# A hybrid decoder step: the first expert matrix transposed on chip beside the branches, so that 128 tokens fetch its rows and VectorE forms their products

## What is computed

```python
x = x + jnp.sum(gates * bproj, axis=2) @ w_out
x = x + peer(rmsnorm(x, norm_ffn), pk_wq, pk_k1, pk_k2, pk_u, pk_v)

def block(xb):                                   # peer, per block of 128 tokens
    q = (xb @ w_q).reshape(PK_BLOCK, PK_HEADS, 2, PK_DKEY // 2)
    s1 = jnp.einsum('thd,kd->thk', q[:, :, 0], sub_k1)
    s2 = jnp.einsum('thd,kd->thk', q[:, :, 1], sub_k2)
    v1, i1 = lax.top_k(s1, PK_TOPK)
    v2, i2 = lax.top_k(s2, PK_TOPK)
    ...
    top, pos = lax.top_k(cand, PK_TOPK)          # 16 of 256 sums, 8 heads: 128 experts a token
    eidx = jnp.take_along_axis(cidx, pos, axis=-1)
    gate = jax.nn.softmax(top, axis=-1)
    act = jax.nn.gelu(jnp.einsum('thkd,td->thk', u_tab[eidx], xb), approximate=False)
    return jnp.einsum('thk,thkd->td', gate * act, v_tab[eidx])
```

## Time and profile before

| what | value |
|---|---|
| median of 3 runs | 2785.19 us (2784.17 to 2786.49) |
| profiled execution, its own time | 2789.63 us |
| its span | 2787.7 us |
| TensorE busy | 2554.8 us, 92% of the span |
| VectorE busy | 1493.1 us, 54% |
| ScalarE busy | 801.3 us, 29% |
| GpSimd busy | 352.9 us, 13% |
| mean granted TensorE clock | 0.945 of full |

### The profile page before, as it was taken

The page is one execution under the profiler, slowest core; times in us unless marked ns, Lnnn a source line. Parts: engine busy times, 40 slices in busy tenths (PEclk is TensorE's granted clock), DMA queues, the critical chain, the costliest instruction groups (busy, mean ns, idle before and its releaser), DMA issues.

```text
span 2787.7 us, 46563 instructions
## 1 busy us (share of the span) xinstructions
PE 2554.8 (92%) x19385; PEld 2379.8 (85%) x19385; DVE 1493.1 (54%) x3427; ACT 801.3 (29%) x1147; POOL 352.9 (13%) x372
## 2 busy tenths in 40 slices
PE   7976886877769999998999999999999999999997
PEld 5954666865548998786999999999999999999997
DVE  3354375426222222376677566666412468778876
ACT  3221252210112112122232344444422333333332
POOL 2000000000000000000000000000000546667520
PEclk9987898978778999998999999999999999999998
DMA  4110320001313332220333346555644789999993
GB/s 133 48 38 23 96 62 2 4 4 48 122 45 87 81 83 85 62 79 23 136 132 136 132 137 190 169 165 165 182 151 148 268 277 341 353 345 345 344 348 122
DMA packets 267010, 398.09 MB, mean 143 GB/s; under 512 B 18641, under 2 KB 192737, under 8 KB 265265
## 3 DMA queue, kind: packets, MB, share of 16 engines
q1 hardware_dynamic: 222960, 274.07, 30.5%
q0 software_dynamic: 25408, 85.38, 8.4%
q10 hardware_dynamic: 18432, 35.66, 3.5%
HBM read 325.13 MB, written 69.92 MB: 142 GB/s over the span
## 4 chain that ended last, share of the span: by engine, by line
PE 87%; DVE 9%; issue 2%; ACT 2%; DMA 0%; DVEq 0%; ACTq 0%
PE PS L988 87%; DVE arena L1545 3%; ACT arena L644 1%; DVE arena L1557 1%; PE PS L992 1%; DVE arena L1739 1%; DVE rstd L1885 1%; ACT arena L648 0%; DVE arena L1551 0%; DVE rstd L1573 0%; DVE arena L1554 0%; ACT L644 0%; DMA XT<-in_xT 0%; DVE arena L1900 0%; DMA arena<-in_memkT 0%
## 5 line engine op out<-in xcount | busy, mean ns | idle before, releaser
L2007 DVE TENSOR_TENSOR LO<-RAW,HI 128x1024 fp32r<-128x1024 f32 x256 | 314.7, 1230 | 511.9 <-ACT HI L911 504.0
L911 ACT ACTIVATE HI<-RAW 128x1024 fp32r<-128x1024 f32 x256 | 271.0, 1059 | 918.5 <-PE PS L988 891.0
L988 PE MATMUL PS<-XH,HI 128*128 128x272 f32 x2048 | 429.2, 291 | 13.8 <-DVE LO L2007 13.8
L988 PE MATMUL PS<-XH,LO 128*128 128x272 f32 x2048 | 424.9, 289 | 0.0
L988 PE MATMUL PS<-XL,HI 128*128 128x272 f32 x2048 | 423.2, 288 | 0.0
L988 PE MATMUL PS<-HT,W 128*128 128x272 f32 (+1 forms) x1536 | 376.8, 407 | 18.6 <-DVE HT L1576 12.4
L988 PEld LDWEIGHTS PS<-HT,W 128*128 128x128 f32 (+1 forms) x1536 | 293.7, 193 | 95.7 <-issue 24.0
L988 PE MATMUL PS<-WH,HI 128*128 128x416 f32 x1024 | 360.0, 352 | 0.0
L988 PE MATMUL PS<-WL,HI 128*128 128x416 f32 x1024 | 359.3, 351 | 0.0
L988 PE MATMUL PS<-WH,LO 128*128 128x416 f32 x1024 | 357.2, 349 | 0.0
L988 PEld LDWEIGHTS PS<-XH,HI 128*128 128x128 f32 x2048 | 322.5, 189 | 14.1 <-issue 14.1
(11 more groups left out here) (272 smaller groups left out, 2940.6 us busy)
## 6 DMA issues: line engine op xcount, KB each, us to landing
RAW<-in_uT SPq DMA_DIRECT2D x128, 512.0 KB
RAW<-in_vT SPq DMA_DIRECT2D x128, 512.0 KB
table_a<-AX ACTq DMA_DIRECT2D x128, 272.0 KB, 2.1
W<-in_w_in SPq DMA_DIRECT2D x58, 512.0 KB, 4.0
gate_table<-GST SPq DMA_DIRECT2D x13, 2048.0 KB, 11.3
AIN<-table_a SPq DMA_DIRECT2D x128, 208.0 KB
GQ<-gate_table SPq DMA_DIRECT2D x32, 832.0 KB
W<-in_wq SPq DMA_DIRECT2D x16, 512.0 KB, 3.9
```

Source lines behind the costliest of these rows:

```text
L911: nc.scalar.activation(HI[:, s % NRING], RAW[:, s % NRING], ACT.Copy).then_inc(S("hi"), 1)
L988: return nc.tensor.matmul(out, lhsT, rhs, start=first, stop=last)
L2007: dve.tensor_tensor(LO_[:, s % NRING], RAW[:, s % NRING], HI[:, s % NRING].bitcast(F32), ALU.subtract).then_inc(S("lo"), 1)
```

## The change

- **Rows of u.** 128 tiles of u are loaded once more, on GpSimd's queue, turned on VectorE in blocks of 32x32 (`turn_tile`, one transpose of 128x1024), and written by GpSimd to a new table `u_rows` in DRAM (`turn_tiles`: four DMAs per tile, each from 32 partitions, in pieces of 1 KB). 18 tiles are turned in the mLSTM, 16 in the RWKV chunks, 10 in attention, 56 beside the gates and 28 beside the queries. One buffer in and one out serve the first two stages, two and two the others. Within each stage GpSimd does its tiles before the stage's other transfers (in the mLSTM before all outputs).
- **First pass for 416 tokens.** 24 matmuls of 416 columns per slot in the place of 48 of 272. The 128 tokens' own vectors are turned to rows (product `xt`, into XTOK); GpSimd gathers 128 rows of u for each (`gather_first`, three buffers), VectorE multiplies and sums (`dot`), ScalarE applies GELU (`picked`). `gather_act` goes.
- **One-hots split.** VectorE compares four tokens at once (two TENSOR_TENSOR of 128x512 per unit), ScalarE multiplies by the gates (`gated_hots`, four activations of 128x128 per unit). 104 units lie in 58 slots from slot 53 on (46 slots with two units, 12 with one) where it was two in each of 52. The parts of the choice take 10 slots per token tile, where it was 8; 16 dots lie beside them, the other 112 behind.
- Constants move into a block that is given up after the branches; some semaphores are merged.

```diff
+TILES = {"M": (0, 18, 1), "R": (18, 16, 1), "A": (34, 10, 2), "G": (44, 56, 2), "Q": (100, 28, 2)}
 def part_slot(t, part):
-    return 2 + 8 * t + part
+    return 2 + 10 * t + part
 def hots_slot(u):
-    return part_slot(NPT, 4) + u // 2
+    return part_slot(NPT - 1, 7) + 4 + u * 58 // (8 * NEB)
+def dotted_by(s):
+    first, even, early = part_slot(0, 7) + 5, part_slot(NPT - 1, 7) + 5, 16
+    if s < even:
+        return max(0, s - first) * early // (even - first)
+    return min(P, early + (s - even) * (P - early) // (NK - 2 - even))
...
 # GpSimd
+            def turn_tiles(phase):
+                first, n, depth = TILES[phase]
+                for i in range(first, first + n + depth):
+                    k = i - depth
+                    if k >= first:
+                        pool.wait_ge(S("tr"), k + 1)
+                        rows, turned = u_rows[k].rearrange("(b c) q x -> q c b x", b=4), tile_out[phase][(k - first) % depth]
+                        for q in range(4):
+                            pool.dma_start(rows[q], turned[32 * q:32 * q + 32].rearrange("c (b x) -> c b x", b=4)
+                                           ).then_inc(S(f"tout{k % 2}"), 16)
+                    if i < first + n:
+                        pool.dma_start(tile_in[phase][(i - first) % depth], a["uT"][:, i].rearrange("p k n -> p (k n)")
+                                       ).then_inc(S(f"tin{i % 2}"), 16)
+                for i in range(2):
+                    pool.wait_ge(S(f"tout{i}"), 64 * ((first + n + 1 - i) // 2))
+            turn_tiles("M")
             pool.wait_ge(S("ctail"), 8)
             pool.dma_start(o["conv"], CT).then_inc(S("out"), 16)
...
+            def gather_first(j):
+                if j >= NGU:
+                    pool.wait_ge(S("dot"), j - NGU + 1)
+                pool.indirect_dma_start(out=GU[j % NGU][0:NGT], out_offset=None, in_=flat_u,
+                                        in_offset=bass.IndirectOffsetOnAxis(ap=EIDX[0:NGT, 1, j:j + 1], axis=0)
+                                        ).then_inc(S(f"gr{j % NGU}"), 16)
...
 # ScalarE
+            def gated_hots(u):
+                act.wait_ge(S("oheq"), u + 1)
+                for x in range(4):
+                    hot = OH[:, u % NOH, 1, x]
+                    ins = nc.scalar.activation(hot, hot, ACT.Copy, scale=IT[:, 2, 4 * u + x:4 * u + x + 1])
+                ins.then_inc(S("oh1"), 1)
...
+                for u in units_at(hots_slot, s):
+                    gated_hots(u)
                 for u in units_at(copy_slot, s):
                     copy_unit(u)
...
 # TensorE, first_products
-                    ins = exact(ps, (HI[:, s % NRING, ks], LO_[:, s % NRING, ks]), (XH[:, k, :], XL[:, k, :]),
-                                k == 0, k == DT - 1)
+                    mul(ps, uh, XH[:, k, :], k == 0, False)
+                    mul(ps, uh, XL[:, k, :], False, False)
+                    ins = mul(ps, ul, XH[:, k, :], False, k == DT - 1)
...
 # VectorE
+            def turn_tile(phase):
+                ...
+                dve.wait_ge(S(f"tin{i % 2}"), 16 * (i // 2 + 1))
+                k = i - depth
+                if k >= first:
+                    dve.wait_ge(S(f"tout{k % 2}"), 64 * (k // 2 + 1))
+                x, y = tile_in[phase][(i - first) % depth], tile_out[phase][(i - first) % depth]
+                dve.transpose(y.rearrange("p (b k r) -> p b k r", b=4, k=DT), x.rearrange("p (k b r) -> p b k r", k=DT, b=4)
+                              ).then_inc(S("tr"), 1)
...
+                turn_tile("M")
+            for _ in range(6):
+                turn_tile("M")
             ps = take(dve, "gt")
...
-                for x in range(4):
-                    a_, b_, g_ = [IT[:, r, 4 * u + x:4 * u + x + 1] for r in range(3)]
-                    dve.tensor_scalar(OH[:, u % NOH, 0, x], iota[:], a_, None, ALU.is_equal)
-                    ins = dve.tensor_scalar(OH[:, u % NOH, 1, x], iota[:], b_, g_, ALU.is_equal, ALU.mult)
-                ins.then_inc(S("oh1"), 1)
+                for i in range(2):
+                    ins = dve.tensor_tensor(OH[:, u % NOH, i], bc(iota[:], 1, 4), bc(IT[:, i, 4 * u:4 * u + 4], 2, P), ALU.is_equal)
+                ins.then_inc(S("oheq"), 1)
+            def dot(j):
+                ...
+                dve.tensor_tensor_reduce(out=row, in0=row, in1=XTOK[0:NGT], scale=1.0, scalar=0.0, op0=ALU.mult, op1=ALU.add,
+                                         accum_out=ACTG[0:NGT, j:j + 1]).then_inc(S("dot"), 1)
```

More of the change, by code:

```diff
@@ L66 @@
 NGR = 6
+NGU = 3
+TILES = {"M": (0, 18, 1), "R": (18, 16, 1), "A": (34, 10, 2), "G": (44, 56, 2), "Q": (100, 28, 2)}
+assert sum(n for _, n, _ in TILES.values()) == NK
 PTILES = [(ND, NGT)] + [(c, min(P, ND - c)) for c in range(0, ND, P)]
@@ L71 @@
 HALF = T // 2
+NCBLK = 2088
 AREN = 28400
@@ L191, in units_at, with dot_slot @@
     return [u for u in range(8 * NEB) if slot_of(u) == s]
+def dotted_by(s):
[3 more added lines that the diff above has]
+    return min(P, early + (s - even) * (P - early) // (NK - 2 - even))
+def dot_slot(j):
+    return min(s for s in range(NK) if dotted_by(s + 1) > j)
 def gathered_by(e):
@@ L281, in hybrid_layer @@
         EIDX = sb("EIDX", [P, 2, P], U32)
-        assert NAX * T + 3 * ND + 5 * P <= DT * T
-        sb("HTrest", [P, DT * T - NAX * T - 3 * ND - 5 * P])
+        GU = [sb(f"GU{i}", [P, D]) for i in range(NGU - 1)]
+        spare = NCBLK + DT * T - NAX * ND - 3 * ND - 5 * P - (NGU - 1) * D
+        assert spare >= 0
+        sb("spare", [P, spare])
         HI, LO_ = [sb(n, [P, NRING, DT * P], F32R) for n in ("HI", "LO")]
-        XH, XL = [sb(n, [P, DT, T], F32R, part) for n in ("XH", "XL")]
+        XH, XL = [sb(n, [P, DT, ND], F32R, part) for n in ("XH", "XL")]
+        OH = sb("OH", [P, NOH, 2, 4, P], stack=part)
+        part.close()
+        sb("XHL", [P, 2 * DT * ND], stack=part)
+        TQ = sb("TQ", [P, 4, D], stack=part)
         part.close()
@@ L619, in _ @@
             pool.wait_ge(S("eidx"), 2)
+            for j in range(P):
+                gather_first(j)
+            pool.wait_ge(S("dot"), P)
             pool.wait_ge(S("pu"), NK)
-            for j in range(NGR):
+            for j in range(P):
                 gather_row(j)
-            for i in range(NAX):
-                pool.wait_ge(S(f"st{i}"), 16 * (NK // NAX))
-            for j in range(EB):
-                gather_act(j)
-            for j in range(P):
-                if j + EB < P:
-                    gather_act(j + EB)
-                if j + NGR < P:
-                    gather_row(j + NGR)
         @block.scalar
@@ L887, in _ @@
                     both(f"pq{i}", QT[:, i % 3, :], ACT.Copy, S("pqe"))
+                if i == 0:
+                    ps = take(act, "xt")
+                    turned = [ps[:, x].rearrange("t (k q r) -> t k q r", k=4, q=4) for x in range(2)]
+                    into = XTOK[:].rearrange("t (q k r) -> t k q r", q=4, k=8)
+                    f(into[:, 0:4], turned[0], ACT.Copy)
+                    out_of("xt", into[:, 4:8], turned[1], ACT.Copy)
                 if i:
@@ L962, in _ @@
                         exp_gates(t)
+                for u in units_at(hots_slot, s):
+                    gated_hots(u)
                 for u in units_at(copy_slot, s):
                     copy_unit(u)
+                for g in range(P // EB):
+                    if s == dot_slot(EB * (g + 1) - 1) + 1:
+                        picked(g)
             act.wait_ge(S("fin"), 1)
@@ L1457, in _ @@
                     project(f"pq{i}", ht, ready=None if i else 2 * DT)
+                if i == 0:
+                    ps = room("xt")
+                    for k in range(DT):
+                        ins = turn(ps[:, k // 4, (k % 4) * P:(k % 4 + 1) * P], HT[:, k, ND:T])
+                    ins.then_inc(mm, 1)
                 if i:
@@ L1915, in _ @@
             for h in range(MH):
-                tt(XM[:, h], bc(XQ[:, h, TP:T], 1, NB), bmask[:], sem=S("xm") if h == MH - 1 else None)
+                tt(XM[:, h], bc(XQ[:, h, TP:T], 1, NB), bmask[:], sem=S("masked") if h == MH - 1 else None)
+            for _ in range(6):
+                turn_tile("A")
             for h in range(MH + 1):
@@ L2178, in _ @@
                     one_hots(u)
+                for j in range(dotted_by(s), dotted_by(s + 1) if s < NK else 0):
+                    dot(j)
                 for j in range(gathered_by(e), gathered_by(e + 1)):
```

115 lines of the change are left out of this document (70 added, 45 removed).

## The result

The changed kernel takes 2802.31 us (median of 4 runs, 2801.72 to 2806.99), the kernel before beside it 2785.84 us (4 runs). The ratio is 1.0064, with a 95% interval of 1.0046 to 1.0081: slower by 0.6%, where the forecast was 2728, faster by 2%. (2802 lies inside the stated range of 2668 to 2824, on the side of its rival of the long loop.) The profiled execution has a span of 2800.9 us, 13.2 more than before.

A forecast was written before the change was run, and what follows sets the result against it. The prediction took TensorE, with 87% of the span, as the bound. It set 131 us won in the first pass against 74 us lost to tiles, -57 from the median 2785.2, giving 2728 us, range 2668 to 2824.

The forecast's parts named there:

- rival of the long loop: Tile turning ahead of the first pass: load behind four writes lands after 7 us, loop 10.5 us, 2833 us; chance 0.17.
- The tile loop, 7.35 us: One-buffer tile turning: signal and four issues 2.3, load 3.8, transpose 1.25, so 7.35 us from transpose to transpose.
- the load, I take 3.8: Load of the next 512 KB tile on GpSimd's queue: 3.8 us, from 5.09 us for 1 MB with the queue free.
- RWKV, +24: RWKV chunks: 3.6 us lost in each of three pairs and 13 in the last pair, together 24 us.
- The queries, +7: Queries: two transposes per round, rounds of 9.35 us (eight) and 8.8 (six); the end moves by 7 us.
- Parts of the choice: First pass, choice of experts: VectorE's work with LO and dots fills 40 of 45 us in ten slots, and holds.
- Gathers, 0: First pass behind slot 54: gathers have over 8 us while one-hots are made, so no loss taken.
- The ring, 7.6 us: First pass, two-unit slots: HI, LO, one-hots, scaling and copies wait on each other, 7.6 us against TensorE's 6.3.
- The rival that it does not bind: First pass: the ScalarE and VectorE cycle does not limit two-unit slots; pass 677 us, kernel 2669; chance 0.13.
- the plain sum's -190: First pass, TensorE taken alone: 4.53 us slots, 190 us less, a pass of 677 us.
- The end of mLSTM +13: End of mLSTM: four outputs issued only after the 18th tile's writes, barrier at 298.6 instead of 285.7, 13 us more.
- The sign set for it: Start of the first pass: forecast 1387 us; a start after 1440 would show the forecast wrong through the tile loop.

The follow-up runs named there:

- the reordered copies: Changed kernel with ScalarE's two copies of gate units placed ahead of the eight activations that scale the one-hots, in the same slot: 2737.2 us.
- the last kernel: Changed kernel with copies before scaling, tiles spread, loads before writes, row products in gaps, one tile inside top16, fourth gather buffer: 2620.48 us, ratio 0.9401 to the kernel before.

## Why the prediction was wrong, point by point

The direction was wrong: -57 forecast, +13 in the profile. The mechanisms of the forecast are in the trace, with two left out (a wait for loads in the queries, and transposes in RWKV's path that were taken as covered); four terms were mis-sized, all to the same side.

- **The tile loop, 7.35 us.** It measured 8.80. The step that failed is "the load, I take 3.8": it was worked out from a load on a free queue with nothing else under way, and for that it holds (3.8 at the median without the writes). On the mean of the thirteen loops the load took 5.1 to the next transpose: 4.4 to landing even without writes, with loads of weights beside some of them, and 5.0 behind four writes. The signal was 0.29, not 0.1. Thirteen loops at 1.45 more are the 19 us by which mLSTM missed (+57.4 against +37).
- **RWKV, +24.** It took +37.1. Pairs of chunks follow each other in 43.3 and 42.7 us (first transposes at 538.87, 582.19 and 624.91), 6.5 more than the 36.5 before (494.93 to 531.47), where I had 3.6. Some 1.0 of these 2.9 us is the longer loop (547.74 to 556.12 is 8.38). Most of the rest is in transposes that I took as covered: the fourth, 1.25 us at 566.75, lies in the chain of waits. In the last pair three loops took 25.7 us instead of 22.1.
- **The queries, +7.** They took +21. VectorE's work alone costs 2 us there (165.5 without writes, rounds of 9.08 and 8.58), less than the 9.35 and 8.8 that I added up. The other 19 are waits for loads, which I left out: behind up to eight writes the loads land after 4.9 to 7.3 us, and a round took 10.4 on the mean.
- **Parts of the choice, "tight, but it holds".** 40 of 45 us on the mean of ten slots, yet the long parts stand in three neighbouring slots, 4.5 us beside LO's 1.14, and a product more is over the slack. 9.3 us. The turned picks took some 6, not 4 (248.5 us to the Gelu of slot 52 without products there, less 53 x 4.53, 0.9 from a product's end to its Gelu, and 1.5 of slow start); 3.5 of them are TensorE's wait. The start was slow in the changed kernel too: its first 77 matmuls took 16.44 us, 1.8 more than at 0.19 each, and the granted clock was 0.72 from 1433.7 to 1440, after 34.7 us without a matmul, and 1.00 from 1440 to 1450.
- **Gathers, 0.** In the changed kernel nearly right: in slots 53 to 112 the pass took 5 us more than my sum of the ring (429.4 against 46 x 7.6 + 12 x 5.45 + 2 x 4.53 = 424), and 4 more at its end, where the chain of waits runs through gathers of 8 to 10 us. They bind as soon as the slots are shorter or hold two products.
- **The ring, 7.6 us.** Right at 7.66 by luck, since two of its pieces were wrong against each other; that it binds is shown by the reordered copies. The rival that it does not bind gave a pass of 677 for TensorE alone: in the last kernel, with the ring gone, it is 682.5, so the plain sum's -190 measured -184.
- **The end of mLSTM +13, gates and output with attention +6, the second pass 0, the transpose 1.25**: right.
- **The rival of the long loop** named the cause, but set it at 10.5 us and had it decide from 9.6. With the queries at +21 and the pass at 758 it decides from less: losses of 121 stand against 108 at 8.8. The point of decision was worked out with all other terms at their favourable values, and so was too high, and its chance of 0.17 too low. The sign set for it, a pass that begins after 1440, was too late for the same reason: the pass began at 1433.7, and the kernel was slower.

On descriptors: in the changed kernel GpSimd's four writes took 2.19 us at 113.00, with VectorE in 128x512 TENSOR_SCALAR and SCALAR_TENSOR_TENSOR instructions, and as much at 147.74, with VectorE idle. The first of the four was issued while a TENSOR_SCALAR ran, took 0.56 us in both places, and landed after 2.6 and 2.4 us. If the TENSOR_SCALAR is a two-port operation, the Trainium skill, SBUF — State Buffer, "DVE blocks DMA", would have the descriptors held up until it ends. No hold-up of a size that matters here is in the trace, so the forecast was right to leave it out; whether the instruction was a two-port operation the trace does not tell, so the rule itself was not tested.

## What to carry to other kernels

A load through one buffer costs its whole loop wherever tiles follow each other and nothing else fills the time, and next to nothing where the same tile stands in a gap of the engine that turns it: the same 34 tiles cost 94 us in one order and none in another, so count gaps against the loop before choosing the places. Take a transfer's time from a row in which it has the same neighbours as it will have, on its own queue and beside it, and compare medians with medians. When an engine both feeds a chain and waits for it (ScalarE: HI, then scaling), put work that is already due into that wait, but look what that work is itself behind: the same copies one slot later cost 137 us, and in their own slot they gave 65.

## What was not expected of the hardware

A 512 KB load on GpSimd's queue landed in 3.8 us at the median alone and in 4.6 behind four writes of 128 KB each in pieces of 1 KB, issued just ahead of it. Put ahead of the writes instead, it landed in 4.3, and the writes went from 2.7 to 3.5, so the loop shortened by 1.3 us and not by the 2.2 of the four issues.

The DMA engines carried 272 GB/s at a share of 0.89 beside the gates, against 346 at 0.95 in the second pass. The pieces of 1 KB are not the cause: the kernel without writes has 179 GB/s at 0.58 in the same stage (890 to 1180 us), the same share for each byte, and the kernel before has 81 at 0.30, more. What makes a byte dearer in this stage was not separated. TensorE lost only some 5 us to it.
